# A hybrid block on one core: block inversion two units earlier, ten short-convolution taps inside the delta rule, the long convolution's taps mostly after it, and z in eight buffers

## The chip, the core and the metric

The kernel runs on one core of a Trainium2 chip. The metric is the device time in microseconds (us) from start to end of one execution; lower is better. The five engines are TensorE (PE), VectorE (DVE), ScalarE (ACT), GpSimd (POOL) and SyncE (SP, which only issues the weight loads here).

## The reference, cut to what matters

Two blocks run one after the other on a sequence of 512 tokens of width 1024, all in float32. The first block (feed-forward, sparse and windowed attention, feed-forward) is not touched by the change. The second block has two layers, and each layer computes

```
h    = rms_norm(x)
proj = h @ w_in       # qkv 1536, z_a 512, a 8, b 8, cf_val 512, cf_glu 512, z_b 512, gate 2048
qkv  = silu(conv5(qkv))                       # five taps, depthwise, centred
q, k = l2_normalize(q), l2_normalize(k)
g    = -exp(a_log) * softplus(a + dt_bias);  beta = sigmoid(b)
o    = gated_delta(q, k, v, g, beta) + the same on the reversed sequence
o    = rms(o) * dn_norm_w * silu(z_a);        y_a = o @ w_dn_out
u    = conv31(cf_val * sigmoid(cf_glu)) + cf_conv_b      # 31 taps, depthwise
u    = silu(layer_norm(u)) * silu(z_b);       y_b = u @ w_cf_out
x    = x + (sigmoid(gate_a) * y_a + sigmoid(gate_b) * y_b) @ w_out
```

The gated delta rule needs, for every chunk of 128 tokens and each of four heads and two directions, the inverse of a unit lower-triangular matrix built from the keys, the decays and beta.

## The kernel before, in words

**Units.** All weights are streamed as 300 units of 128x1024 float32 through a ring of four buffers (`raw`). ACT rounds a unit to a high part (`whi`, line 928), POOL makes the low part (`wlo`, line 2027), and PE multiplies with three matmuls for each 128x128 tile (lines 378 to 380): 24 matmuls for a unit of eight tiles. A layer of the second block has 60 units: 8 for the gated linear unit (`glu`) of the long convolution, 12 for qkv, 16 gates, 8 for z, 8 for the two output matrices, 8 for `w_out`.

**Order.** Every engine has its own hand-written program, and engines meet only at semaphores. In a layer, PE does the eight glu units, then the twelve qkv units `j = 0..11` in the order `QKV_ORDER` (keys, queries, values). Each qkv unit lands in one of four PSUM banks; DVE runs its five taps out of that bank into `acc` (lines 1835 and 1838), and ACT applies Silu and, for keys and queries, squares the result; PE adds the squares up over the rows (`sum_rows`, line 405), ACT takes Ln and Exp (`l2_roots`, lines 1186 and 1189), and DVE scales (`unit_length`, line 1768).

**Inversion.** After unit 8 PE forms running sums of the decays and the products of keys by keys (lines 715 to 717 and 689). After unit 10 it spreads the picked decays and beta (`pick`, `pick_b`, lines 727 and 729). DVE then builds 32x32 diagonal blocks (`exponents`, `block_matrices`, from line 1797), and inverts all 32 blocks at once in thirty steps `eliminate(u)` of two small instructions each (lines 1811 and 1813). Between the steps it scales the queries (`u == 8`) and prepares the first decays (`u == 16`, line 1908). `inverse_blocks` (line 1817) and `start_inverse` (line 1932) hand the result to PE, whose first use of it is the transpose of line 835.

**Delta rule.** Meanwhile PE runs six gate units (`LEAD_UNITS`). Then `delta` works through four chunks `i = 0..3`, both directions side by side, and fills PE's waits with tiles of ten more gate units at nine named points of a chunk. DVE has at each of these points a number of taps of the long convolution (`conv(point)`, `POINT_TAPS`). In a chunk with `i > 0`, DVE scales the transposed inverse (line 1956), runs the taps of the point `decay`, and then makes the decayed keys (line 1915), for which PE waits at line 807.

**Long convolution.** 31 taps on four channel groups. The fourth group is ACT's and POOL's (lines 1142 and 2063). The other three, 93 taps, are DVE's (line 1711, each 128x512 out of SBUF): 20 in the glu stage (`GLU_TAPS`), 8 behind the qkv units (`QKV_PHASE_TAPS`), 56 at the points of the four chunks, and 9 behind the last chunk.

**After the delta rule.** PE runs the z units. Behind z unit 0 it sums the convolved rows for the layer norm's mean (line 405, `cu`), behind z unit 1 the squares of `o` and then of the centred `cu`. ACT's Silu of a z unit goes into one of two `prod` buffers, so that ACT waits for `z_used` from the third unit on. z_b comes before z_a, and PE's first output unit in `merge` reads the `cu` half of the rows first.

Of the kernel before, what the change touches and what calls it, by code (L numbers as in the profile page):

```python
# [15 lines left out]
P = 128  # L16
# [42 lines left out]
for _name, _n in (("norm", 8), ("qkv_w", 12 * QKV_TAPS), ("cf_w", 4 * CF_TAPS), ("cf_b", 4), ("ln_w", 4),  # L59
# [95 lines left out]
    "outer": (221824, [P, 256], F32),  # L155
    "fh": (141952, [P, 8, S], F32R),
# [158 lines left out]
POINT_TAPS = {"decay": 2, "level1": 2, "join1": 2, "level2": 1, "join2": 2, "last": 1, "keys": 2, "out": 2}  # L315
LEAD_UNITS = 6
# [48 lines left out]
QKV_PHASE_TAPS = [LATER_TAPS[j:j + 1] if j < 8 else [] for j in range(12)]  # L365
DELTA_TAPS = LATER_TAPS[8:]
# [3 lines left out]
def tensor_engine(pe, m, s):  # L370
# [264 lines left out]
    def merge(g):  # L635
# [4 lines left out]
        for c in range(KD):  # L640
# [4 lines left out]
            for r in (0, 1) if mixer else (1, 0):  # L645
                for k in range(4):
                    if c == 0:
                        pe.wait_ge(s.mix_lo, 8 * g + 4 * (r if mixer else 1 - r) + k + 1)
# [16 lines left out]
    def layer(l):  # L665
# [27 lines left out]
        for j in range(12):  # L693
# [17 lines left out]
            if j == 8:  # L711
# [9 lines left out]
            if j == 10:  # L721
                pe.wait_ge(s.kk_read, 2 * l + 1)
                keys_by_keys(ps[:, 5, :], 3).then_inc(s.d_kk)

                pe.wait_ge(s.picked, l + 1)
                for d in range(2):
                    pe.matmul(ps[:, 6 + d, :], mat(m, "quad"),
                              m.pick[:, 16 * d:16 * d + 16, :].rearrange("p b c -> p (b c)"), start=True, stop=True)
                pe.matmul(ps[:, 4, :], mat(m, "quad"), m.pick_b[:].rearrange("p b c -> p (b c)"), start=True,
                          stop=True).then_inc(s.d_pre)  # L730
        for n in range(LEAD_UNITS):
# [88 lines left out]
    def delta(l):  # L820
# [6 lines left out]
        for i in range(NT):  # L827
# [78 lines left out]
def scalar_engine(act, m, s):  # L906
# [244 lines left out]
    def layer(l):  # L1151
# [23 lines left out]
        def qkv_silu(j):  # L1175
            act.wait_ge(s.qconv, 12 * l + j + 1)
            act.activation(m.qkv[:, QKV_ORDER[j], :], m.acc[:, j % 2, :], ACT.Silu).then_inc(s.qkv)
            if j < 8:
                act.wait_ge(s.qkv, 12 * l + j + 1)
# [17 lines left out]

        for j in range(12):
            weights_upto(u0 + L_QKV + j + AHEAD + 1)
            if j:  # L1200
                qkv_silu(j - 1)
# [15 lines left out]
            if j == 9:  # L1217
                act.wait_ge(s.cum, l + 1)
                cum = m.dsm[:, 0].rearrange("p t (d n) -> p d t n", d=2)
                act.copy(cum, ps[:, 4, 0:32].rearrange("p (d t n) -> p d t n", d=2, t=NT))  # L1220
                act.copy(m.dsm[:, 1], ps[:, 4, 32:64].rearrange("p (t n) -> p t n", t=NT)).then_inc(s.cum_s)
                act.wait_ge(s.d_kk, 8 * l + 2 * l + 1)
                for t in range(3):
                    ins = diagonal_blocks(t, 5 + t)
                ins.then_inc(s.kk_read)
            if j == 11:
                act.wait_ge(s.d_min, 9 * l + 1)
                act.activation(m.blk_l[:], m.blk_l[:], ACT.Exp).then_inc(s.d_dec)
                act.wait_ge(s.d_kk, 8 * l + 2 * l + 2)
                diagonal_blocks(3, 5).then_inc(s.kk_read)  # L1230
        qkv_silu(11)
        for n in range(LEAD_UNITS):
            weights_upto(u0 + L_GATE + n + AHEAD + 1)
            if n == 0:
                l2_roots(4, (0, 1, 2, 3))
# [10 lines left out]
        def z_unit(n):  # L1246
# [3 lines left out]
            if n >= 2:  # L1250
                act.wait_ge(s.z_used, 8 * l + n - 1)
            act.activation(m.prod[:, n % 2, :], ps[:, Z_BANKS[n % 3], :], ACT.Silu).then_inc(s.filled)
# [6 lines left out]
        weights_upto(u0 + L_Z + 1 + AHEAD + 1)  # L1259
        for c in range(4):  # L1260
            act.wait_ge(s.cu_c, 4 * l + c + 1)
            act.activation(m.dl[:, 0, c, :], m.cu[:, c, :], ACT.Square).then_inc(s.cu_sq)
        weights_upto(u0 + L_Z + 2 + AHEAD + 1)
        for c in range(4):
            act.wait_ge(s.o_sums, 4 * l + c + 1)
            act.activation(ps[:, c, :], ps[:, c, :], ACT.Ln, bias=eps, scale=1.0 / P)
        act.wait_ge(s.var, l + 1)
        then(act.activation(ps[:, 5, :], ps[:, 5, :], ACT.Ln, bias=eps, scale=1.0 / (4 * P)))
        for c in range(4):
            act.activation(ps[:, c, :], ps[:, c, :], ACT.Exp, scale=-0.5).then_inc(s.o_root)  # L1270
        act.activation(ps[:, 5, :], ps[:, 5, :], ACT.Exp, scale=-0.5).then_inc(s.root_cu)

        def split_rows(k):
            src = m.o[:, k, :] if k < 4 else m.cu[:, k - 4, :]
            act.wait_ge(s.z_used, 8 * l + (k + 5 if k < 4 else k - 3))
            act.copy(m.fh[:, k, :], src).then_inc(s.mix_hi)

        for n in range(8):
            z_unit(n)
            if n == 1:  # L1280
                for c in range(4):
                    act.wait_ge(s.cu_n, 4 * l + c + 1)
                    act.activation(m.cu[:, c, :], m.cu[:, c, :], ACT.Silu, bias=lcl(m, l, "ln_b", c),
                                   scale=lcl(m, l, "ln_w", c)).then_inc(s.cu_silu)
            if n:
                split_rows(n + 3 if n < 5 else n - 5)
        weights_upto(u0 + L_OUT + AHEAD + 1)
        split_rows(3)
# [13 lines left out]
    def delta(l):  # L1302
# [15 lines left out]
        for i in range(NT):  # L1318
# [4 lines left out]
            for lv in range(1, nl):  # L1323
# [3 lines left out]
                fill(i, f"level{lv}")  # L1327
                fill(i, f"join{lv}")
# [34 lines left out]
def vector_engine(dve, m, s):  # L1363
# [304 lines left out]
    def layer(l):  # L1668
# [153 lines left out]
        for j in range(12):  # L1822
# [459 lines left out]
```

## Time and profile before

| what | value |
|---|---|
| time, median of 3 runs | 2229.32 us (2227.79 to 2230.11) |
| the profiled execution's own time | 2232.36 us |
| its span, first to last instruction | 2231.0 us |
| PE busy | 2091.9 us, 94% of the span |
| DVE busy | 1276.0 us, 57% |
| ACT busy | 873.1 us, 39% |
| POOL busy | 895.9 us, 40% |
| mean granted clock of TensorE | 0.974 of full speed |

The profiled execution is 1.4 us longer than its span and 3.0 us longer than the median of the three runs. Layer 0 of the second block begins near 1240 us of the span and layer 1 near 1740 us; the two look alike instruction by instruction, and times below are of layer 0 unless layer 1 is named. A clock of 1.00 is TensorE's 2.4 GHz, 0.50 is 1.2 GHz.

### The profile page before, as it was taken

Reading aid. Unit: us, or ns where it says so; the run is one execution under the profiler, and the core shown is the slowest. Engines: PE = TensorE matmul, PEld = TensorE weight load, DVE = VectorE, ACT = ScalarE, POOL = GpSimd, SP = SyncE. Lnnn points to the kernel's source line nnn. Section 1 sums busy time; section 2 is a strip of 40 time slices with the busy share of each in tenths; the row PEclk is TensorE's granted clock in tenths of the full one; section 3 lists DMA queues with packets and bytes.
Section 4 is the critical chain, followed back from the end, with each engine's and each line's share of the span. In section 5 each row is a group of like instructions: output and inputs, shape, how many; then the busy total and the mean of one; then the engine's idle time right before and its main releaser. Section 6 shows DMA issues by size and latency. Waiting matters only on the chain.

```text
span 2231.0 us, 26548 instructions
## 1 busy us (share of the span) xinstructions
PE 2091.9 (94%) x10668; PEld 1670.5 (75%) x10668; DVE 1276.0 (57%) x1943; ACT 873.1 (39%) x1404; POOL 895.9 (40%) x431
## 2 busy tenths in 40 slices
PE   7999999989999999999999899889999999799997
PEld 5888787766656788888787677678788777688785
DVE  4422223775677533222225999887543899887543
ACT  4222233313444543222235376344533375343532
POOL 4444443421213344444444454344344454343342
PEclk9999999998999999999999999999999999899999
DMA  4333232320101233333332222100232222010232
GB/s 150 107 132 97 93 95 83 126 66 26 32 22 56 67 98 95 101 95 95 92 96 85 67 76 66 39 25 24 76 95 86 87 83 67 29 30 25 79 96 76
DMA packets 46185, 169.08 MB, mean 76 GB/s; under 512 B 5232, under 2 KB 6000, under 8 KB 45808
## 3 DMA queue, kind: packets, MB, share of 16 engines
q1 hardware_dynamic: 45344, 165.60, 23.9%
q8 instruction: 85, 1.39, 0.3%
q10 hardware_dynamic: 720, 1.79, 0.2%
q14 instruction: 36, 0.29, 0.0%
HBM read 165.27 MB, written 2.10 MB: 75 GB/s over the span
## 4 chain that ended last, share of the span: by engine, by line
PE 71%; DVE 19%; ACT 6%; issue 2%; DMA 1%; POOL 0%; ACTq 0%; DVEq 0%
PE ps L378 20%; PE ps L379 19%; PE ps L380 19%; DVE cu L1711 4%; DVE acc L1838 2%; DVE blk_t L1813 1%; PE ps L405 1%; DVE outer L1811 1%; PE ps L568 1%; PE ps L584 1%; PE ps L553 1%; PE ps L850 1%; PE ps L807 1%; PE ps L497 1%; DVE rt L1694 1%
## 5 line engine op out<-in xcount | busy, mean ns | idle before, releaser
L2027 POOL TENSOR_TENSOR wlo<-raw,whi 128x1024 fp32r<-128x1024 f32 x300 | 739.1, 2470 | 944.6 <-ACT whi L928 943.8
L378 PE MATMUL ps<-xh,whi 128*128 128x512 f32 x1600 | 654.4, 409 | 28.5 <-POOL wlo L2027 17.1
L380 PE MATMUL ps<-xh,wlo 128*128 128x512 f32 x1600 | 628.1, 393 | 0.0
L379 PE MATMUL ps<-xl,whi 128*128 128x512 f32 x1600 | 627.8, 392 | 0.0
L378 PEld LDWEIGHTS ps<-xh,whi 128*128 128x128 f32 x1600 | 303.2, 190 | 116.9 <-issue 28.3
L928 ACT CAST whi<-raw 128x1024 fp32r<-128x1024 f32 x300 | 312.7, 1044 | 190.6 <-DMA raw<-in_stream 190.5
L380 PEld LDWEIGHTS ps<-xh,wlo 128*128 128x128 f32 x1600 | 302.9, 189 | 65.6
L379 PEld LDWEIGHTS ps<-xl,whi 128*128 128x128 f32 x1600 | 303.5, 190 | 64.5 <-issue 7.0
L1711 DVE SCALAR_TENSOR_TENSOR cu<-up,lcols,cu 128x512 f32<-128x512 f32 x180 | 188.4, 1089 | 0.1
L1447 DVE TENSOR_TENSOR ml<-mid,mh 128x512 fp32r<-128x512 f32 x42 | 61.3, 1464 | 164.4 <-ACT mh L984 164.4
L2063 POOL TENSOR_TENSOR cu<-cu,prod 128x512 f32<-128x512 f32 x60 | 87.3, 1455 | 160.5 <-ACT prod L1142 159.3
L378 PE MATMUL ps<-mh,whi 128*128 128x512 f32 x336 | 132.5, 394 | 12.1 <-DVE ml L1447 6.1
L1438 DVE TENSOR_TENSOR ups<-ps,rn 128x512 f32<-128x512 f32 x44 | 30.4, 691 | 194.4 <-PE ps L380 194.4
L974 ACT ACTIVATE sil<-sil 128x512 f32<-128x512 f32 x44 | 27.8, 632 | 285.2 <-DVE sil L1436 285.2
L379 PE MATMUL ps<-ml,whi 128*128 128x512 f32 x336 | 131.9, 393 | 0.0
L380 PE MATMUL ps<-mh,wlo 128*128 128x512 f32 x336 | 131.7, 392 | 0.0
L378 PE MATMUL ps<-fh,whi 128*128 128x512 f32 x256 | 102.3, 400 | 10.7 <-POOL wlo L2027 9.5
L379 PE MATMUL ps<-fl,whi 128*128 128x512 f32 x256 | 100.9, 394 | 0.0
L380 PE MATMUL ps<-fh,wlo 128*128 128x512 f32 x256 | 100.7, 393 | 0.0
L1436 DVE TENSOR_TENSOR sil<-ps,rn 128x512 f32<-128x512 f32 x44 | 30.4, 691 | 117.2 <-PE ps L380 117.1
L378 PEld LDWEIGHTS ps<-mh,whi 128*128 128x128 f32 x336 | 63.8, 190 | 27.0 <-issue 13.7
L378 PE MATMUL ps<-m_y,whi 128*128 128x512 f32 x192 | 74.7, 389 | 0.0
(342 smaller groups left out, 3059.2 us busy)
## 6 DMA issues: line engine op xcount, KB each, us to landing
raw<-in_stream SPq DMA_DIRECT2D x300, 512.0 KB, 3.6
w1k<-in_w SPq DMA_DIRECT2D x1, 2048.0 KB, 8.2
w1v<-in_w SPq DMA_DIRECT2D x1, 2048.0 KB, 10.2
outT<-h SPq DMA_DIRECT2D x4, 512.0 KB, 2.7
h<-in_xT ACTq DMA_DIRECT2D x2, 512.0 KB, 7.7
h<-in_xT SPq DMA_DIRECT2D x2, 512.0 KB, 7.6
mats<-in_mats ACTq DMA_DIRECT2D x1, 448.0 KB, 10.7
msk<-in_masks SPq DMA_DIRECT2D x1, 258.0 KB, 3.9
```

Of the source, the lines that this page charges most:

```text
L378: pe.matmul(out, wh, hi, start=first, stop=False)
L379: pe.matmul(out, wh, lo, start=False, stop=False)
L380: return pe.matmul(out, wl, hi, start=False, stop=last)
L928: act.copy(m.whi[:, slot, :], m.raw[:, slot, :]).then_inc(s.whi)
L974: act.activation(m.sil[:, i % 2, :], m.sil[:, i % 2, :], ACT.Silu).then_inc(s.sil)
L1436: dve.tensor_tensor(m.sil[:, p, :], ps[:, 2 * p, :], m.rn[:], ALU.mult).then_inc(s.g_scaled)
L1438: dve.tensor_tensor(m.ups[:, p, :], ps[:, 2 * p + 1, :], m.rn[:], ALU.mult).then_inc(s.u_scaled)
L1447: dve.tensor_tensor(lo, m.mid[:, i, :], hi.bitcast(F32), ALU.subtract).then_inc(s.ml)
L1711: ins = dve.scalar_tensor_tensor(out=dst, in0=src, scalar=w, in1=dst, op0=ALU.mult, op1=ALU.add)
L1838: ins = dve.scalar_tensor_tensor(out=acc[:, first:last], in0=src[:, first + k - QKV_PAD:last + k - QKV_PAD], scalar=w, in1=acc[:, first:la ...
L2027: pool.tensor_tensor(m.wlo[:, slot, :], m.raw[:, slot, :], m.whi[:, slot, :].bitcast(F32), ALU.subtract).then_inc(s.wlo)
L2063: pool.tensor_tensor(m.cu[:, 3, :], m.cu[:, 3, :], m.prod[:, k % 2, :], ALU.add).then_inc(s.shared)
```

## The change

- Unit 8's PE products move behind unit 7, and those of unit 10 behind unit 8 (the last keys product into bank 3). `pick_rows` moves from behind unit 9's taps to before unit 8's, and `exponents` directly behind unit 8's taps.
- The taps of unit 9 are run inside the elimination at `u == 5`. Units 10 and 11 are copied raw by ACT to their place in `qkv`, and their ten taps run out of SBUF at the points of chunk 0 (`LATE_TAPS`). ACT applies their Silu there.
- Queries are scaled at `u == 12` instead of 8, and the first decays prepared at `u == 20` instead of 16. POOL's identity matrices of chunk 0 move from behind the scaling of the queries to the qkv stage.
- Long-convolution taps: 9 in the glu stage instead of 20, none behind the qkv units instead of 8, 49 at the points of the chunks instead of 56 (chunk 0 gives its first four points to the late taps), and 35 behind the last chunk instead of 9. Together 93 as before.
- In chunks 1 to 3 the decayed keys come before the taps of `decay`.
- z_a comes before z_b, each z unit has its own buffer (`z_o`, `z_cu`), and `merge` reads the `o` half first. The mean of the long convolution is taken behind z unit 3 instead of 0, its variance behind z unit 5 instead of 1.

```diff
@@ constants
+    "z_o": (158336, [P, 4, S], F32),
+    "z_cu": (215680, [P, 4, S], F32),
+LATE_TAPS = {"decay": 2, "level1": 3, "join1": 3, "level2": 2}
+UNIT_Q, DECAY_EXP = 12, 20
@@ tap_plan
-    for c, n in enumerate((1, 2, 10, 7)):
+    for c, n in enumerate((1, 2, 4, 2)):
-QKV_PHASE_TAPS = [LATER_TAPS[j:j + 1] if j < 8 else [] for j in range(12)]
-DELTA_TAPS = LATER_TAPS[8:]
+DELTA_TAPS = LATER_TAPS
@@ PE, layer
-            if j == 8:
+            if j == 7:
                 pe.wait_ge(s.gl, l + 1)
                 pe.wait_ge(s.l2, 8 * l + 4)
...
+            if j == 8:
+                pe.wait_ge(s.qconv, 12 * l + 8)
+                keys_by_keys(ps[:, 3, :], 3).then_inc(s.d_kk)
+                pe.wait_ge(s.picked, l + 1)
+                pe.matmul(ps[:, 4, :], mat(m, "quad"), m.pick_b[:].rearrange("p b c -> p (b c)"), start=True, stop=True)
+                pe.wait_ge(s.kk_read, 2 * l + 1)
+                for d in range(2):
+                    ins = pe.matmul(ps[:, 6 + d, :], mat(m, "quad"),
...
             if j == 10:
-                pe.wait_ge(s.kk_read, 2 * l + 1)
-                keys_by_keys(ps[:, 5, :], 3).then_inc(s.d_kk)
...
+                pe.wait_ge(s.kk_read, 2 * l + 2)
@@ PE, z units
         z_unit(0)
-        pe.wait_ge(s.conv, 3 * l + 3)
-        pe.wait_ge(s.shared, 30 * l + 30)
-        sum_rows(ps[:, 4, :], [m.cu[:, c, :] for c in range(4)]).then_inc(s.mean)
         z_unit(1)
         for c in range(4):
             pe.wait_ge(s.o_sq, 4 * l + c + 1)
             sum_rows(ps[:, c, :], [m.rt[:, c, :]]).then_inc(s.o_sums)
+        z_unit(2)
+        z_unit(3)
+        pe.wait_ge(s.conv, 3 * l + 3)
+        pe.wait_ge(s.shared, 30 * l + 30)
+        sum_rows(ps[:, 5, :], [m.cu[:, c, :] for c in range(4)]).then_inc(s.mean)
+        z_unit(4)
+        z_unit(5)
         pe.wait_ge(s.cu_sq, 4 * l + 4)
...
@@ ACT
+        def raw_values(j):
+            act.wait_ge(s.unit, u0 + L_QKV + j + 1)
+            act.copy(m.qkv[:, QKV_ORDER[j], :], ps[:, j % 4, :]).then_inc(s.qkv)
...
+        qkv_silu(9)
+        raw_values(10)
+        raw_values(11)
@@ DVE, layer
-        for j in range(12):
+        for j in range(9):
             if j == 7:
                 for n in range(4):
                     unit_length(n, (6, 7, 5, 4)[n])
...
+            if j == 8:
+                pick_rows()
+            qkv_taps(j)
...
+        exponents()
         block_matrices()
+        dve.wait_ge(s.cum_s, 3 * l + 2)
+        dve.tensor_scalar(m.dsm[:, 2], m.dsm[:, 2], -1.0, None, ALU.mult).then_inc(s.cum_d)
         for u in range(1, BASE - 1):
             eliminate(u)
-            if u == 6:
...
-            if u == 8:
+            if u == 5:
+                qkv_taps(9)
+            if u == UNIT_Q:
                 for n in range(4):
                     unit_length(4 + n, n)
-            if u == 16:
+            if u == DECAY_EXP:
                 decay_exponents(l, 0)
@@ DVE, delta
+        late = [(j, n) for j in (10, 11) for n in range(QKV_TAPS)]
         def conv(point):
+            if late:
+                for j, n in late[0:LATE_TAPS[point]]:
+                    qkv_tap(j, n)
+                del late[0:LATE_TAPS[point]]
+                return
...
                 if lv == 1:
-                    conv("decay")
                     if i:
                         decayed_keys(l, i)
+                    conv("decay")
```

On DVE, in layer 0, the end of the qkv stage reads before as follows (`pick` and `pick_b` are `pick_rows`, the first group of `acc` is unit 10, the second unit 11, `blk_l` and `blk_t` are the blocks to be inverted):

```order
L1781 TENSOR_TENSOR pick<-dsm,mats 128x512 x2
L1782 TENSOR_TENSOR pick_b<-small,mats 128x512
...
L1835 TENSOR_SCALAR acc<-ps,lcols 128x512
...
L1790 TENSOR_TENSOR blk_l<-dsm,ps 128x512
L1791 TENSOR_TENSOR blk_l<-ps,dsm 128x512
L1792 TENSOR_SCALAR blk_l<-blk_l 128x1024
L1835 TENSOR_SCALAR acc<-ps,lcols 128x512
...
L1797 TENSOR_TENSOR blk_l<-blk_l,small 128x512
L1798 TENSOR_TENSOR blk_l<-blk_l,ps 128x512
L1803 SCALAR_TENSOR_TENSOR blk_l<-kk,blk_l 128x1024
L1804 STREAM_TRANSPOSE blk_t<-blk_l 128x1024
```

In the changed kernel the same place, where the only group of `acc` is unit 8, reads:

```order
L1873 TENSOR_SCALAR acc<-ps,lcols 128x512
...
L1825 TENSOR_TENSOR blk_l<-dsm,ps 128x512
L1826 TENSOR_TENSOR blk_l<-ps,dsm 128x512
L1827 TENSOR_SCALAR blk_l<-blk_l 128x1024
L1832 TENSOR_TENSOR blk_l<-blk_l,small 128x512
L1833 TENSOR_TENSOR blk_l<-blk_l,ps 128x512
L1838 SCALAR_TENSOR_TENSOR blk_l<-kk,blk_l 128x1024
L1839 STREAM_TRANSPOSE blk_t<-blk_l 128x1024
L1905 TENSOR_SCALAR dsm<-dsm 128x32
```

The taps of units 9, 10 and 11 no longer stand ahead of the blocks. On DVE at the end of the last chunk, before (`rt` is the state, `o` the output, `cu` the long convolution), we have:

```order
L1990 TENSOR_TENSOR rt<-rt,ps 128x512
L1711 SCALAR_TENSOR_TENSOR cu<-up,lcols,cu 128x512 x11
L1875 SCALAR_TENSOR_TENSOR cu<-ps,cu 128x512 x4
L1879 SCALAR_TENSOR_TENSOR o<-o,lcols,ps 128x512 x4
L1883 TENSOR_TENSOR cu<-cu,ps 128x512 x4
```

and in the changed kernel:

```order
L2058 TENSOR_TENSOR rt<-rt,ps 128x512
L1746 SCALAR_TENSOR_TENSOR cu<-up,lcols,cu 128x512 x37
L1920 SCALAR_TENSOR_TENSOR o<-o,lcols,ps 128x512 x4
L1942 SCALAR_TENSOR_TENSOR cu<-ps,cu 128x512 x4
L1931 TENSOR_TENSOR o<-o,z_o 128x512 x4
```

There are 37 taps in a row (two of the point `out`, 35 left over) instead of 11, and the centring of `cu`, which needs PE's mean, comes behind the scaling of `o`.

## Rows read from the trace of the kernel before

**Rows 1.** Waits of PE from 1300 us on: total, times, longest.

```profile
PE ps L835 <- DVE dl L1932: 19.6, 2, 10.0
PE ps L807 <- DVE rt L1915: 18.6, 6, 3.1
```

**Rows 2.** PE timeline: start, length, engine, line, operation [idle before, releaser].

```profile
1278.85 0.47 PE L378 MATMUL ps<-xh,whi 128*128 128x512 f32 x1 [1.06 <-POOL wlo L2027]
...
1292.04 1.12 PE L405 MATMUL ps<-rt,mats 128*128 128x512 f32 x2 [2.04 <-ACT rt L1181]
...
1329.59 0.37 PE L715 MATMUL ps<-small,mats 128*128 128x16 f32 x2 [0.22 <-DVE qkv L1768]
...
1344.39 1.16 PE L689 MATMUL ps<-qkv 128*128 128x128 f32 x8 [0.29 <-ACT kk L1195]
...
1371.10 2.07 PE L795 MATMUL ps<-mats,small 128*128 128x128 f32 x8 [2.94 <-DVE qkv L1768]
...
1409.31 1.97 PE L835 MATMUL ps<-mats,dl 128*128 128x128 f32 x8 [9.66 <-DVE dl L1932]
...
1788.73 1.12 PE L405 MATMUL ps<-rt,mats 128*128 128x512 f32 x2
...
1905.77 0.47 PE L835 MATMUL ps<-mats,dl 128*128 128x128 f32 x1 [9.96 <-DVE dl L1932]
```

**Rows 3.** Windows: length, busy PE, PEld, DVE, ACT, POOL, granted clock, DMA.

```profile
1371.00:1377.00 6.00, 5.90 (x27) 5.91 (x28) 5.79 (x8) 0.55 (x1) 3.88 (x2) 0.50 0.04 15
1378.00:1399.00 21.00, 21.00 (x94) 17.37 (x93) 19.93 (x40) 9.57 (x12) 8.01 (x5) 1.00 0.27 75
1451.00:1454.00 3.00, 0.15 (x5) 0.18 (x7) 3.00 (x4) 0.47 (x1) 3.00 (x2) 1.00 0.00 0
...
1532.00:1537.00 5.00, 5.00 (x44) 4.54 (x45) 4.03 (x5) 1.39 (x3) 1.44 (x1) 0.50 0.01 3
```

**Rows 4.** DVE timeline, from the last short-convolution units to the inverse.

```profile
1340.51 3.10 DVE L1838 SCALAR_TENSOR_TENSOR acc<-ps,lcols,acc 128x510 f32<-128x510 f32 x4
...
1357.64 0.68 DVE L1797 TENSOR_TENSOR blk_l<-blk_l,small 128x512 f32<-128x512 f32 x1
...
1372.71 2.40 DVE L1813 TENSOR_TENSOR blk_t<-blk_t,outer 128x198 f32<-128x198 f32 x1
...
1404.35 1.90 DVE L1817 STREAM_TRANSPOSE blk_w<-blk_t 128x1024 f32<-128x1024 f32 x1
```

**Rows 5.** ACT timeline: Silu of unit 5, and Exp of the keys' roots.

```profile
1318.59 0.63 ACT L1177 ACTIVATE qkv<-acc 128x512 f32<-128x512 f32 x1
...
1325.52 2.05 ACT L1189 ACTIVATE ps<-ps 128x512 f32<-128x512 f32 x4
```

**Rows 6.** DVE timeline in chunks 1 (first three) and 3.

```profile
1450.51 2.60 DVE L1711 SCALAR_TENSOR_TENSOR cu<-up,lcols,cu 128x512 f32<-128x512 f32 x2
1453.02 1.28 DVE L1915 SCALAR_TENSOR_TENSOR rt<-ps,dl 128x512 f32<-128x512 f32 x2
...
1459.47 1.35 DVE L1967 COPY_PREDICATED dl<-levels,ps 128x512 f32<-128x512 uint8 x2
...
1538.02 0.69 DVE L1922 TENSOR_TENSOR dl<-ps,dl 128x512 f32<-128x512 f32 x1 [1.46 <-PE ps L850]
```

**Rows 7.** DVE, POOL and PE timelines behind the last chunk.

```profile
1563.63 11.68 DVE L1711 SCALAR_TENSOR_TENSOR cu<-up,lcols,cu 128x512 f32<-128x512 f32 x11
...
1570.38 2.40 POOL L2027 TENSOR_TENSOR wlo<-raw,whi 128x1024 fp32r<-128x1024 f32 x1 [3.08 <-ACT whi L928]
...
1579.36 3.60 PE L405 MATMUL ps<-cu,mats 128*128 128x512 f32 x8
...
1634.67 0.50 PE L378 MATMUL ps<-fh,whi 128*128 128x512 f32 x1 [0.58 <-DVE fl L1895]
```

**Rows 8.** DVE's groups from 1276 to 1361 us: count, busy, mean ns.

```profile
L1711 DVE SCALAR_TENSOR_TENSOR cu<-up,lcols,cu 128x512 f32<-128x512 f32 x15 | 20.2, 1377 | 0.0
```

More of the change, by code:

```diff
@@ L1258, in layer @@
             act.activation(m.rt[:, c, :], m.o[:, c, :], ACT.Square).then_inc(s.o_sq)
-        weights_upto(u0 + L_Z + 1 + AHEAD + 1)
+        z_unit(0)
+        z_unit(1)
+        for c in range(4):
+            act.wait_ge(s.o_sums, 4 * l + c + 1)
+            then(act.activation(ps[:, c, :], ps[:, c, :], ACT.Ln, bias=eps, scale=1.0 / P))
+        for c in range(4):
+            act.activation(ps[:, c, :], ps[:, c, :], ACT.Exp, scale=-0.5).then_inc(s.o_root)
+        z_unit(2)
+        z_unit(3)
@@ L1260, in layer @@
+        weights_upto(u0 + L_Z + 4 + AHEAD + 1)
         for c in range(4):
             act.wait_ge(s.cu_c, 4 * l + c + 1)
[L1262 to L1266, printed above, removed]
+            act.activation(m.rt[:, c, :], m.cu[:, c, :], ACT.Square).then_inc(s.cu_sq)
@@ L1267, in layer @@
+        z_unit(4)
+        z_unit(5)
+        for k in range(4):
+            split_rows(k)
+        weights_upto(u0 + L_Z + 6 + AHEAD + 1)
         act.wait_ge(s.var, l + 1)
         then(act.activation(ps[:, 5, :], ps[:, 5, :], ACT.Ln, bias=eps, scale=1.0 / (4 * P)))
+        act.activation(ps[:, 5, :], ps[:, 5, :], ACT.Exp, scale=-0.5).then_inc(s.root_cu)
+        z_unit(6)
         for c in range(4):
[L1270 removed]
@@ L1271, in layer @@
[L1271 to L1286, printed above, removed]
+            act.wait_ge(s.cu_n, 4 * l + c + 1)
@@ L1287, in layer @@
+            act.activation(m.cu[:, c, :], m.cu[:, c, :], ACT.Silu, bias=lcl(m, l, "ln_b", c),
+                           scale=lcl(m, l, "ln_w", c)).then_inc(s.cu_silu)
+        z_unit(7)
         weights_upto(u0 + L_OUT + AHEAD + 1)
-        split_rows(3)
+        for k in range(4, 8):
+            split_rows(k)
     def decays(l, i):
@@ L1327, in delta @@
                 fill(i, f"level{lv}")
+                if i == 0:
+                    j = 9 + lv
+                    act.wait_ge(s.qconv, 12 * l + j + 1)
+                    act.activation(m.qkv[:, QKV_ORDER[j], :], m.acc[:, j % 2, :], ACT.Silu).then_inc(s.qkv)
                 fill(i, f"join{lv}")
@@ L2063, in shared_tap, with chunk, identities @@
             pool.tensor_tensor(m.cu[:, 3, :], m.cu[:, 3, :], m.prod[:, k % 2, :], ALU.add).then_inc(s.shared)
+    def chunk(l, i):
+        return [(d, 8 * l + 2 * i + d, delta_buffers(m, d), i if d == 0 else NT - 1 - i) for d in range(2)]
+    def identities(l, i):
+        for d, at, b, t in chunk(l, i):
+            if i:
+                pool.wait_ge(s.d_vn, at - 1)
+            else:
+                pool.wait_ge(s.qkv, 14 * l + 1)
+            pool.tensor_copy(b.T, all_heads(mat(m, "ident"))).then_inc(s.d_t0)
     def delta(l):
@@ L2073, in delta @@
         for i in range(NT):
-            both = [(d, 8 * l + 2 * i + d, delta_buffers(m, d), i if d == 0 else NT - 1 - i) for d in range(2)]
-            for d, at, b, t in both:
-                if i:
-                    pool.wait_ge(s.d_vn, at - 1)
-                else:
-                    pool.wait_ge(s.qkv, 12 * l + 12)
-                    pool.wait_ge(s.l2, 8 * l + 8)
-                pool.tensor_copy(b.T, all_heads(mat(m, "ident"))).then_inc(s.d_t0)
+            both = chunk(l, i)
+            if i:
+                identities(l, i)
+            else:
+                pool.wait_ge(s.l2, 8 * l + 8)
             for d, at, b, t in both:
```

183 lines of the change are left out of this document (100 added, 83 removed).

## The prediction

> **What bounds the kernel now.** I read the page for the shares, then PE's waits over the second block, then the timelines of PE and DVE at the places those waits name, then the granted clock around them. PE is busy 94% of the span and the two layers are the only part the change touches, so a gain can only come from PE's idle time there and from the slow clock behind it. The waits show where it sits: 19.6 us in two waits at line 835 for the inverse, and 18.6 us in six waits at line 807 for the decayed keys [rows 1]. The reader is to see that each of the first two is almost 10 us long, one in each layer [rows 2], and that DVE, not PE, ends last there. Smaller ones: 2.94 us at 1371.10 for the scaled queries, 2.04 us at 1292.04 for the first keys' squares, 1.06 us for a weight unit [rows 2]. Idle time costs more than itself: behind the 2.94 us wait the granted clock is 0.50 for at least 6 us, behind a 3.1 us wait of chunk 3 it is 0.50 for at least 5 us, while behind the like wait of chunk 1 it stays 1.00 [rows 3]. A stretch of 5 to 6 us at 0.50 gives away 2.5 to 3 us of PE work.
>
> **Term 1: the inverse is ready earlier.** In full stretches PE runs 94 recorded matmuls in 21 us [rows 3]; a few records are missing, so I take 5.45 us for a unit of 24. A row sum adds 0.9 us (8 records in 3.6 us [rows 7]), so a unit with one takes 6.35.
> Eleven long-convolution taps leave the glu stage and eight the qkv stage. DVE is then free when unit 0 ends and follows PE instead of trailing it, so the waits of 2.04 and 1.06 us go, and unit 2 ends at 1292.04 - 2.04 - 1.06 = 1288.9. Units 3 to 5 with their sums end at 1308.0; the fourth sum and unit 6 make 1314.3, unit 7 1319.8.
> The keys must now be scaled behind unit 7, one unit sooner. A unit's five taps take 3.10 us for four [rows 4] and about 0.75 for the first: 3.85. Unit 5's taps end at 1311.9. From its Silu to the end of the roots' Exp ACT takes 1327.57 - 1318.59 = 9.0 us [rows 5], so the roots are there at 1320.9. DVE's four scalings then end between 1321.5 and 1323; I take 1322.4. PE waits 2.6 us where it waited 0.22 [rows 2]. Behind it stand units 8 to 11 and everything else.
> Then, on PE: from 1329.59 to 1344.39 stand the products and two units less 0.29 us of wait [rows 2], so the products take 3.6 us: 1326.0. Unit 8: 1331.5. The last keys product (1.16 us [rows 2]) and three 128x512 products of two passes at 0.9 each: 1335.4. On DVE three instructions of about 0.65 each make the exponents: 1337.4. ACT's table load and Exp, which I estimate from the four-instruction Exp of 2.05 us [rows 5] at 2.4 together, end at 1339.8. So `block_matrices` starts at 1339.8 where it started at 1357.64 [rows 4].
> From there to the transposes of line 1817 DVE took 1404.35 - 1357.64 = 46.7 us [rows 4]. The change adds unit 9's taps, 3.85. It also adds a wait: at u = 12 the queries need roots whose sums stand behind gate unit 0. PE reaches those at 1335.4 + 4 x 5.45 = 1357.2, sums 3.1 us, ACT about 4 us for Ln and Exp, so the roots come near 1363, and I take 2 us of wait, less about 1 us of an old wait for small exponentials. The transposes start at 1339.8 + 46.7 + 3.85 + 1 = 1391.4, and line 835 runs 4.96 us after them as before [rows 2, 4]: 1396.3 instead of 1409.31. **Gain in layer 0: 13.0 us.** PE itself, with gate units 1 to 5 and the first products, arrives near 1391 to 1393, so the wait shrinks to some 3 to 5 us and DVE remains the bound.
> Layer 1: unit 2 ends at 1788.73 with no wait behind DVE [rows 2]. The same 107.4 us lead to 1896.1 instead of 1905.77: **9.7 us.** Together 22.7. The new 2.6 us wait at unit 7 lies between the 2.04 us behind which no slow stretch followed and the 2.94 us that had one; at even odds of losing 2.5 us it costs 1.2 a layer. **Term 1: -20.** Bounds: -28 with no wait at u = 12 and no slow clock, -12 when every GpSimd instruction meets an elimination step. Such a step takes 2.40 us instead of 0.4 [rows 4], and with PE running on there are two or three more weight units inside the elimination than before, 2 us each.
>
> **Term 2: the chunks.** Putting the decayed keys first brings PE's line 807 forward by the two taps, 2.60 us [rows 6], out of 3.1 [rows 1]. I do not book 6 x 2.5 us. In chunk 1 DVE runs from 1450.51 to the copy at 1459.47 without idle [rows 6]; the same instructions stand in that stretch after the swap, so PE waits for that copy (at line 842) instead. Only in chunks 2 and 3 has DVE something to win: there PE came back at 0.50 and DVE in turn waited, 1.46 us at 1538.02 [rows 6] and smaller pieces. That is 2 to 3 us a chunk if the moved wait, now about 2.3 us, leaves the clock alone, and nothing if it doesn't. In chunk 0 DVE has ten short taps where it had seven long ones at the first four points; three more at 0.75 us are 2.3 us, but there too it waited for a slow PE. The V transposes' new wait is for a Silu beside the copy of the inverse and costs under 0.5. I take -2.5 a layer: **Term 2: -5**, bounds -12 and +4.
> Here the Trainium skill, page "SBUF — State Buffer", section "Who interferes with whom", speaks against the change: a VectorE instruction with two SBUF inputs and a GpSimd instruction that reads SBUF exclude each other for the whole instruction, while one with a single SBUF input is not held up. The trace agrees: a POOL instruction of 2.40 us stands beside an elimination step of 2.40 instead of 0.4, and four taps out of PSUM take 3.10 everywhere. The ten late taps of a layer have left PSUM for SBUF. If three of them met a weight unit, at 2.0 us each, term 2 would be +7 for both layers instead of -5.
>
> **Term 3: behind the last chunk.** 37 taps instead of 11. Eleven took 11.68 us from 1563.63, 1.06 each, with two POOL instructions of 2.40 among them [rows 7]. POOL has one weight unit for each PE unit here, so I keep 1.06: 39.3 us, to 1603.0. PE has 18 gate tiles and z unit 0, which end at 1579.36 [rows 7], then z1 (5.45), the sums of `o` (3.2), z2 and z3 (10.9): 1599. It waits about 4 us for the convolution, long enough, by the 2.94 us case, for a slow stretch: 2.5. Then mean 3.1, z4 and z5 10.9, variance 3.2, z6 and z7 10.9: 1603.0 + 28.1 + 2.5 = 1633.6. The first output unit takes 5.45, and waits for the `cu` half: ACT has to finish z7 and a weight cast before it splits, which I put at 1.5 us. It ends at 1640.5. Before, its last tile of 0.68 us began at 1634.67 after 0.58 us of wait [rows 7]: 1635.4. Loss 5.1 us a layer, and half a us for the likelier DVE hold-ups. **Term 3: +11**, bounds +4 (POOL spares the taps, no slow clock) and +18. The eight z buffers are worth the two waits of about 1 and 0.58 us that z units and `merge` had, already inside this sum. Moving POOL's identity copies and reordering z_a and z_b cost nothing: their cover is PE's own units, and without it they would cost the 1.2 us of the copy.
>
> **Sum.** -20 - 5 + 11 = -14. The profiled execution took 2232.36, so 2218 for its like. It lies 3.0 us above the median of the runs shown, so the median should be about **2215 us**.
>
> **The rivals.**
> - *More of it arrives.* The moved waits of about 2.3 us leave the clock at 1.00, as the 3 us of chunk 1 did [rows 3], and the roots don't hold DVE: term 1 -25, term 2 -9, term 3 +9, so 2204. The long slow stretches behind chunk 2 and 3 speak against it.
> - *The start is not gained.* PE's products behind unit 7 wait for ACT's chain, and extra weight units hold the elimination, so that line 835 comes only 7 us sooner in each layer: -14, -2, +12, so 2225. For it: the 2.40 us step [rows 4]. Against: 17.8 us of head start at `block_matrices` stand against 3.85 us of added work.
> - *Slower: the tail becomes the bound.* Everything behind the last chunk waits on the 37 taps. In the qkv stage a tap of the same shape took 1377 ns on average [rows 8], because POOL does its long-convolution adds besides the weights. At that rate 37 taps take 51 us, 11.6 more a layer: 2215 + 23 = 2238. Each 0.1 us a tap is 3.7 us a layer; the change turns to a loss above 1.06 + 14/74 = 1.25 us a tap. Against: POOL's adds for the long convolution are over by then, and the eleven taps behind the last chunk measured 1.06.
> - *It does nothing*, because both gains were cover for DVE work that must be done anyway: DVE does the same work in all, but 57% of the span leaves it idle time, above all behind the chunks, where it waited in the z units. This shares the 2225 to 2234 region with the second rival.
>
> **How the numbers follow.** Near 2215 (2209 to 2221): 0.42. More (2198 to 2209): 0.27. Little at the start (2221 to 2234): 0.22, of which somewhat less than half lies within 0.2% of 2229.3, that is above 2224.9; 0.2% is about what a measurement of this kernel can tell from no change. Slower: 0.09, 0.02 of it from stacked waits short of the tail rival. So faster 0.81, same 0.10, slower 0.09. The range leaves out most of the slow rival and the far end of the fast one: 2202 to 2226.
>
> **What would show it.** Right: PE's wait at the inverse's transposes falls from 9.7 us to 3 to 5 and starts some 13 us (layer 0) and 10 us (layer 1) sooner; a wait of 2 to 3 us behind unit 7; waits near 2.3 us at the second-level transposes instead of 3.1 at the first products in chunks 1 to 3; a PE wait near 4 us before the sum of `cu`. Wrong: an elimination that takes over 52 us, a tail whose taps take other than about 1.06 us, or slow stretches inside the chunks where there was none.

## The result, and the profile after

The changed kernel takes 2237.54 us (median of 18 runs, 2230.25 to 2240.13) and the kernel before, on the same chips, 2229.72 us (18 runs, 2222.76 to 2234.12). The ratio is 1.0031, interval 1.0023 to 1.0040: **slower by 0.3%**, where 2215 us and faster was forecast. The median lies outside the range of 2202 to 2226.

The profiled execution of after took 2233.95 us, 3.6 below its own median, and that of before was 2.6 above its. The two traces differ by only 1.7 us of span, so I read from them where time moves, and take how much from the ratios. PE's waits from 1240 us on: total, times, longest. ([rows 1] counts from 1300 us; its two figures are the same from 1240.)

```profile
PE ps L859 <- DVE dl L2035: 25.3, 7, 4.1
...
PE ps L384 <- ACT sg L1168: 6.0, 2, 3.0
PE ps L852 <- DVE dl L1992: 5.9, 4, 2.1
PE ps L721 <- DVE qkv L1803: 4.7, 2, 2.4
PE ps L384 <- DVE fl L1937: 4.3, 4, 1.9
PE ps L824 <- DVE rt L1975: 3.5, 6, 0.6
```

Line numbers have moved: 835 is now 852, 842 is 859, 807 is 824, and the tap's line 1711 is 1746. The two waits at the inverse fell from 19.6 to 5.9 us and the six at the decayed keys from 18.6 to 3.5. A wait that hardly existed has taken their place: 25.3 us at line 859, the second-level transposes, for DVE's copy at line 2035 (line 1967 before). The 6.0 us at line 384 behind ACT are new too: only 0.5 us stood there before.

PE's timeline at the places that the prediction named, to be held against [rows 2] and [rows 7]:

```profile
1286.86 1.02 PE L411 MATMUL ps<-rt,mats 128*128 128x512 f32 x2
...
1320.17 0.37 PE L721 MATMUL ps<-small,mats 128*128 128x16 f32 x2 [2.36 <-DVE qkv L1803]
...
1384.39 0.47 PE L384 MATMUL ps<-xh,whi 128*128 128x512 f32 x1 [2.98 <-ACT sg L1168]
...
1397.53 0.66 PE L852 MATMUL ps<-mats,dl 128*128 128x128 f32 x4 [2.01 <-DVE dl L1992]
1400.29 1.11 PE L852 MATMUL ps<-mats,dl 128*128 128x128 f32 x4 [2.10 <-DVE dl L1992]
...
1452.90 1.94 PE L859 MATMUL ps<-mats,dl 128*128 128x128 f32 x8 [4.08 <-DVE dl L2035]
...
1598.25 2.31 PE L411 MATMUL ps<-cu,mats 128*128 128x512 f32 x5
...
1631.76 0.75 PE L384 MATMUL ps<-fh,whi 128*128 128x512 f32 x1 [1.90 <-DVE fl L1937]
```

PE's transposes of the inverse (line 852) start at 1397.53 instead of 1409.31. At 1598.25 PE reaches the sum of `cu` without waiting. What happens between is in the windows of chunks 1, 2 and 3, first the kernel before, then after. Columns: length, then busy time and count of PE, PEld, DVE, ACT, POOL, then granted clock, DMA.

```profile
1444.08:1482.39 38.31, 34.85 (x313) 30.65 (x312) 32.74 (x55) 17.49 (x31) 17.15 (x11) 1.00 0.08 28
1482.39:1522.21 39.82, 36.35 (x313) 32.04 (x312) 32.59 (x55) 17.48 (x31) 16.96 (x11) 0.96 0.09 28
1522.21:1561.18 38.97, 35.52 (x303) 31.41 (x302) 31.45 (x53) 16.86 (x30) 14.68 (x8) 0.91 0.09 28
```

```profile
1434.73:1477.57 42.84, 37.15 (x314) 32.42 (x312) 35.42 (x55) 17.48 (x31) 16.50 (x11) 0.92 0.08 25
1477.57:1518.91 41.34, 36.32 (x313) 31.72 (x312) 34.63 (x55) 17.48 (x31) 16.79 (x11) 0.96 0.09 27
1518.91:1560.30 41.39, 35.70 (x304) 30.98 (x303) 34.15 (x53) 16.88 (x30) 14.13 (x8) 0.92 0.09 26
```

DVE runs the same 55, 55 and 53 instructions and is busy 7.4 us longer with them. In chunk 1 the clock falls from 1.00 to 0.92 besides; in chunks 2 and 3 it is as before. The DVE timeline of chunk 1 shows which instructions grew; [rows 6] has the same place before.

```profile
1439.96 1.28 DVE L2024 TENSOR_TENSOR dl<-ps,small 128x512 f32<-128x512 f32 x2
1441.16 1.28 DVE L1975 SCALAR_TENSOR_TENSOR rt<-ps,dl 128x512 f32<-128x512 f32 x2
1442.35 7.11 DVE L1746 SCALAR_TENSOR_TENSOR cu<-up,lcols,cu 128x512 f32<-128x512 f32 x4
...
1452.04 1.33 DVE L2035 COPY_PREDICATED dl<-levels,ps 128x512 f32<-128x512 uint8 x2
```

And POOL's timeline of after, beside it:

```profile
1440.24 2.53 POOL L2161 TENSOR_TENSOR dl<-dl,qkv 128x512 f32<-128x512 f32 x2 [9.80 <-ACT dl L1326]
1442.72 2.81 POOL L2095 TENSOR_TENSOR wlo<-raw,whi 128x1024 fp32r<-128x1024 f32 x1
1445.70 3.22 POOL L2131 TENSOR_TENSOR cu<-cu,prod 128x512 f32<-128x512 f32 x2 [0.17 <-ACT prod L1161]
```

Four taps take 7.11 us in one run. POOL works from 1440.24 to 1448.92 with 0.17 us of pause, first the scaled queries, then a weight's low part, then two of its own long-convolution adds. Before, the like adds stood elsewhere, behind the taps, beside DVE's scores:

```profile
1449.59 2.96 POOL L2084 TENSOR_TENSOR dl<-dl,qkv 128x512 f32<-128x512 f32 x2 [9.79 <-ACT dl L1296]
1452.52 2.80 POOL L2027 TENSOR_TENSOR wlo<-raw,whi 128x1024 fp32r<-128x1024 f32 x1
1457.56 3.13 POOL L2063 TENSOR_TENSOR cu<-cu,prod 128x512 f32<-128x512 f32 x2 [2.25 <-ACT prod L1142]
```

From the scaled queries to the adds are 7.97 us before and 5.46 after: with the keys first PE's products are ready sooner, ACT's behind them, and POOL's adds wait only for ACT.

By stages the traces say, after minus before, both layers: to the inverse -17.0 (10.5 and 6.5, counted from the start of the layer's own work, since the two executions were 1.3 us apart there already), chunk 0 +4.4, chunks 1 to 3 +12.7, tail +2.8.

### The profile page after: what moved, and what is told of

It is laid out like the page before. It is cut to its first block, busy times and chain, and to the rows that moved or that the text cites. A ratio compares the mean times of both kernels' runs of the same rounds, so it can differ in the third digit from the quotient of the medians.

```text
span 2232.7 us, 26560 instructions
## 1 busy us (share of the span) xinstructions
PE 2091.1 (94%) x10668; PEld 1668.5 (75%) x10668; DVE 1285.8 (58%) x1943; ACT 896.8 (40%) x1424; POOL 894.5 (40%) x431
## 4 chain that ended last, share of the span: by engine, by line
PE 74%; DVE 16%; ACT 7%; issue 1%; DMA 1%; POOL 0%; ACTq 0%; DVEq 0%
PE ps L384 21%; PE ps L386 20%; PE ps L385 20%; DVE cu L1746 2%; PE ps L411 1%; PE ps L574 1%; PE ps L590 1%; PE ps L559 1%; DVE blk_t L1848 1%; DVE outer L1846 1%; DVE acc L1876 1%; PE ps L503 1%; ACT whi L947 1%; DVE rn L1434 1%; ACT dl L1368 1%
## 5 line engine op out<-in xcount | busy, mean ns | idle before, releaser
L1746 DVE SCALAR_TENSOR_TENSOR cu<-up,lcols,cu 128x512 f32<-128x512 f32 x180 | 193.0, 1126 | 0.1
## 6 DMA issues: line engine op xcount, KB each, us to landing
mats<-in_mats ACTq DMA_DIRECT2D x1, 448.0 KB, 10.5
```

Source lines behind the costliest of these rows:

```text
L1746: ins = dve.scalar_tensor_tensor(out=dst, in0=src, scalar=w, in1=dst, op0=ALU.mult, op1=ALU.add)
```

## The experiments

Theory A: the taps collide with POOL's instructions because the swap leaves four of them in one run. Theory B changes with the experiment: in x1 and x2 the order of the two calls costs nothing, and the late taps or the moved inversion cost the time; in x3 and x9 four taps in one run hold PE up whatever POOL does. Against both stands the forecast's slower rival, the tail. Each kernel's ratio is to the kernel before on the same chip.

**x1: after, the two calls swapped back.**

```
                 if lv == 1:
-                    if i:
-                        decayed_keys(l, i)
                     conv("decay")
+                    if i:
+                        decayed_keys(l, i)
```

> The changed kernel with one part undone: in chunks 1 to 3 the taps of point decay stand ahead of the decayed keys again. Theory A (collision): in the changed kernel the four taps of decay and level1 run together and take 7.11 us where they took 2.60 and 2.30 apart, because the instruction that reads PSUM no longer stands beside POOL's work; undoing it gives about 2 us back in each of six chunks, so about 12 us less than the changed kernel: near 2225 us, or 0.998 of before, with PE's wait back at the first products (3.1 us) and gone from the second-level transposes. Theory B (the late taps or the moved inversion cost it): the order of these two is neutral, the time stays within 2 us of the changed kernel (2235 to 2239, 1.003) and only the place of the wait moves.

2220.95 us, ratio 0.9969 (0.9956 to 0.9982). DVE's timeline of the chunk and PE's wait at the decayed keys are those of before again:

```profile
1438.68 2.59 DVE L1746 SCALAR_TENSOR_TENSOR cu<-up,lcols,cu 128x512 f32<-128x512 f32 x2
1441.19 1.27 DVE L1975 SCALAR_TENSOR_TENSOR rt<-ps,dl 128x512 f32<-128x512 f32 x2
1442.39 2.30 DVE L1746 SCALAR_TENSOR_TENSOR cu<-up,lcols,cu 128x512 f32<-128x512 f32 x2
...
PE ps L824 <- DVE rt L1975: 18.6, 6, 3.1
```

Four taps in 4.89 us instead of 7.11. Without the swap the change is faster by 0.3%.

**x2: before, with the swap alone** (the same edit the other way).

> The kernel before with that one part alone: decayed keys ahead of the taps of decay in chunks 1 to 3. Theory A: the four taps take about 7.1 us instead of 4.9, PE waits about 4 us at the second-level transposes, and the kernel becomes about 8 to 13 us slower than before (1.004 to 1.006). Theory B: no change (0.999 to 1.001). My prediction's own step would have it 5 us faster (0.998).

2247.26 us, ratio 1.0088 (1.0072 to 1.0105): the swap costs 19.6 us in the old kernel, more than the 8 to 13 that theory A expected. Line 807 loses 15.1 us of wait, line 842 gains 24.5, and line 879 goes from 2.1 to 7.2.

```profile
1452.14 7.11 DVE L1711 SCALAR_TENSOR_TENSOR cu<-up,lcols,cu 128x512 f32<-128x512 f32 x4
...
PE ps L842 <- DVE dl L1967: 24.5, 6, 4.1
...
PE ps L807 <- DVE rt L1915: 3.5, 6, 0.6
```

**x3: after, POOL's adds at later points** of each chunk.

```
-SHARED_POINTS = ("level1", "join1", "level2", "join2", "values")
+SHARED_POINTS = ("join2", "last", "keys", "values", "out")
```

> The changed kernel with ACT's and POOL's adds of the fourth channel group moved from the points level1, join1, level2, join2, values to join2, last, keys, values, out. Theory A: with POOL's adds away from it the run of four taps falls from 7.11 to about 5.5 us (POOL's product with the queries and its weight unit remain), PE's wait at the second-level transposes from 4.1 to about 2.5, and the kernel gains 6 to 10 us on the changed one (about 2229, 1.000), unless the adds collide as badly at their new places. Theory B: the run of four taps is long for another reason, and stays at 7 us; no gain.

2225.38 us, ratio 0.9987 (0.9975 to 0.9998). With only the end of the scaled queries and the weight beside them, the four taps take 5.02 us, and the wait at line 859 is halved:

```profile
1443.99 5.02 DVE L1746 SCALAR_TENSOR_TENSOR cu<-up,lcols,cu 128x512 f32<-128x512 f32 x4
...
PE ps L852 <- DVE dl L1992: 15.8, 10, 2.1
PE ps L859 <- DVE dl L2035: 12.0, 6, 2.0
...
PE ps L824 <- DVE rt L1975: 6.8, 6, 1.1
```

But the waits at lines 852 and 824 grew, and over the whole trace these three lines add up to 34.6 us, against 34.7 in after. In chunks 1 to 3 of both layers PE's waits sum to 28.1 us, 3.9 less than in after, while the chunks are 8.4 us shorter. The rest goes with the clock: no single wait there is above 2.0 us instead of 4.1, and the granted clock of the three chunks of layer 0 is 1.00, 1.00 and 0.96 where after has 0.92, 0.96 and 0.92.

**x9: x3 with the calls swapped back,** the fourth corner of the square.

> x3 (POOL's long-convolution adds at later points) with the two instructions swapped back: taps ahead of the decayed keys. It is the fourth corner of a square: swapped or not, POOL's adds early or late. With the adds early the swap cost 16.6 us in the changed kernel (x1 against after). If that cost is the four taps meeting POOL's adds (theory A), the swap is worth little or something with the adds late: PE's waits of 2.0 us at the second-level transposes turn into 3.1 us at the half-level products, chunks become about 1 us longer than x3's 40.4, and the kernel is 0 to 7 us slower than x3: 2225 to 2232. If the swap costs by itself, whatever POOL does (theory B: four taps in one run hold up PE), x9 is some 10 us or more faster than x3: 2215 or below.

2233.73 us, ratio 1.0021 (1.0010 to 1.0033). PE waits 21.8 us at line 824, 3.7 at most, and 11.1 at line 852. At 2229.7 us for before, the square reads: adds early, taps first 2222.8; adds early, keys first 2236.6; adds late, taps first 2234.4; adds late, keys first 2226.8. The swap costs 13.8 us with the adds early and gains 7.6 with them late. Theory B falls. The traces agree: chunks 1 to 3 of both layers together take 238.3, 253.1, 257.0 and 244.7 us, in the same order. Here too the clock carries most of it: x9's chunks are 12.4 us longer than x3's and hold only 2.8 us more of wait, but in layer 0 they run at 0.92, 0.96 and 0.92.

Late adds are not free themselves, and with the taps first they cost 11.6 us. In x3 and x9 POOL's last add of a chunk stands ahead of its identity copies for the next one, and DVE waits 1.71 us for them at 1437.92 (x3) and 1434.92 (x9). In chunks 1 to 3 of x9 PE then waits 7.5 us at line 852, where x1 has no such wait, and 3.2 us more than x1 at line 824, with the lower clock besides. That these waits make up the whole cost is not shown.

**x4: after, with no tap at the two early points** and six at `keys`, behind the last level.

```
-POINT_TAPS = {"decay": 2, "level1": 2, ..., "keys": 2, "out": 2}
+POINT_TAPS = {"decay": 0, "level1": 0, ..., "keys": 6, "out": 2}
```

> The changed kernel with the four taps of decay and level1 moved to the point keys in chunks 1 to 3 (in chunk 0 only the taps behind the late ones change), where DVE waits 4 us for PE. The number of taps is the same. Both theories agree that these taps are on the path ahead of the second-level transposes: the copy there comes 4 to 7 us sooner, the waits of 4.1 us go, and with them the slow clock behind them. Six times 3 to 4.5 us: 2210 to 2219 us, 0.992 to 0.995 of before, unless six taps at keys outlast DVE's 4 us of idle time, which would give back about 1 us a chunk.

2196.43 us, ratio 0.9855 (0.9836 to 0.9874), the fastest of all: 32 us under before, and below the 2210 to 2219 that was expected. Its chunks:

```profile
1435.06:1470.82 35.76, 34.81 (x313) 30.66 (x312) 31.41 (x55) 17.50 (x31) 17.68 (x11) 1.00 0.10 30
1470.82:1506.57 35.75, 34.81 (x313) 30.66 (x312) 31.40 (x55) 17.50 (x31) 17.67 (x11) 1.00 0.10 31
1506.57:1540.50 33.93, 32.99 (x304) 29.09 (x303) 30.23 (x53) 16.88 (x30) 13.72 (x8) 1.00 0.10 32
```

PE is busy 34.8 of 35.8 us, and the clock is 1.00 throughout. In chunk 1 the same 55 instructions keep DVE busy for 31.4 us, 4.0 less than in after. Six taps at `keys` run unhindered:

```profile
1461.31 4.05 DVE L1746 SCALAR_TENSOR_TENSOR cu<-up,lcols,cu 128x512 f32<-128x512 f32 x6
```

That is 0.68 us a tap, so the four of after lost 7.11 - 2.70 = 4.4 us to POOL and the four of before 4.90 - 2.70 = 2.2.

**x5: before, with the same table of taps.**

> The kernel before, with the same table of tap places as x4: no tap at decay and level1, six at keys. Before, chunks 1 to 3 took 38.3, 39.8 and 38.8 us in layer 0, and x4's took 35.8, 35.8 and 33.9. If the four early taps are what holds a chunk in the kernel before as well (theory T), its chunks become as short as x4's: about 4 us each, 24 us in both layers, so near 2205, and x4 stays 7 to 10 us below it, which is what the change's start and tail are worth without the swap. If x4's gain is only the collision taken away, which the kernel before does not have (theory S), this table moves it by less than 5 us: 2223 to 2230.

2206.93 us, ratio 0.9891 (0.9876 to 0.9906), with chunks of 35.8, 35.8 and 33.9 us. 24 us lay open in the old kernel without any of this change. x4 is 0.0036, or 8 us, below it: what the start and the tail of the change are worth when nothing collides. The forecast's first and third terms had -20 + 11 = -9.

**x6: x4 with the old places of the early taps.**

```
-    for c, n in enumerate((1, 2, 4, 2)):
+    for c, n in enumerate((1, 2, 10, 7)):
...
+            if j < 8:
+                cf_tap(*LATER_TAPS[j])
```

> x4 with the old places of the early long-convolution taps: ten and seven in the last two glu units instead of four and two, and one behind each of the first eight qkv units. The tail falls from 33 taps to 14. The taps that leave the tail ended there 5 us before PE came to the sum of cu, so they give nothing back. At the start the waits behind DVE in units 0 to 2 return, about 3 us in layer 0, and DVE reaches the keys' scaling later. Theory of the trace (tail is covered): 3 to 9 us slower than x4, 2199 to 2205. Theory of the prediction (tail costs 5.5 us a layer): the trade is about even or x4 loses up to 6 us: 2190 to 2198.

2212.72 us, ratio 0.9918 (0.9903 to 0.9933), 14 us slower than x4 and so beyond both ranges. The tail went from 33 taps to 14, and in layer 0 the time from the last output product to the first result of `merge` stayed at 75.75 us. The start paid for all of it: PE waits 10.9 us in two waits for the keys' scaling, where x4 has 4.7, and 4.0 in three waits for the keys' squares, where x4 shows none.

```profile
PE ps L721 <- DVE qkv L1803: 10.9, 2, 5.8
```

**x8: x4 with a longer tail,** `keys` 2 instead of 6.

> x4 with two taps at keys instead of six and none added elsewhere: four taps fewer in every chunk, 16 more behind the last chunk (49 instead of 33 in each layer). In x4 33 taps took 30.55 us, 0.93 each, and ended at 1573.5; PE came to the sum of cu at 1578.5. By that rate 16 taps are 14.8 us, less 5.0 us of room: PE waits 9.8 us in each layer, 20 us in both, and 0 to 5 us of slow clock: 2216 to 2221. By the prediction's 1.06 us a tap the 49 take 52 us: 13 to 14 us of wait a layer and 5 of slow clock: 2227 to 2230. If the chunks also gain from having fewer taps, up to 5 us less in each case.

2213.07 us, ratio 0.9920 (0.9905 to 0.9934). DVE's tail, and PE's sum of `cu`:

```profile
1545.88 41.15 DVE L1746 SCALAR_TENSOR_TENSOR cu<-up,lcols,cu 128x512 f32<-128x512 f32 x49
...
1587.08 3.77 PE L411 MATMUL ps<-cu,mats 128*128 128x512 f32 x4 [5.51 <-DVE cu L1746]
```

49 taps are 0.84 us each, less than either rate that I had expected with. PE could have begun at 1581.57, which is 35.7 us behind the first tap: some 42 taps fit. The four matmuls behind the wait take 3.77 us at a mean granted clock of 0.52, where five took 2.31 in after: the wait costs clock too. A tail that is too long does set the end, but the change's 37 taps are not too many.

**x7 and x10: x4 with chunk 0's exponents at step 16 and at step 24** of the elimination instead of 20.

```
-UNIT_Q, DECAY_EXP = 12, 20
+UNIT_Q, DECAY_EXP = 12, 16
```

> x4 with chunk 0's decay exponents at step 16 of the elimination instead of 20. In x4 and in after a gate unit waits 3.0 us behind ACT because the exponents come late. If the inverse alone sets the end of that stretch, this wait is only moved to the inverse's transposes: within 1.5 us of x4's 2196. If the wait also costs clock or delays something behind it, 2 to 6 us faster.

> x4 with chunk 0's decay exponents at step 24 of the elimination instead of 20 (x7 had 16, and its inverse came 4 us later though the same instructions ran: seven of the elimination's instructions took 2.3 to 2.5 us instead of 0.2 to 0.4, beside POOL's weights, where x4 had five). If where the steps fall against POOL's instructions is what decides (theory L), the place of the exponents moves the inverse by 2 us steps in no set direction: 2190 to 2204. If earlier exponents are better for the gate unit that waits for them and later ones worse (theory G), it is 2 to 5 us slower than x4: 2198 to 2201, with a gate unit's wait behind ACT longer than 3.0 us.

x7: 2203.47 us, 0.9874 (0.9857 to 0.9890). x10: 2205.56 us, 0.9893 (0.9874 to 0.9911). x10 loses 8 us to x4. x7's 4 us are no more than the two intervals leave open, but in its trace the transposes of the inverse come 3.9 us later after the keys' scaling than in x4 (2.6 in layer 1), though DVE runs the same instructions. It had been expected level with x4 or faster. DVE's and POOL's timelines of x7 say why:

```profile
1383.76 2.42 DVE L1846 TENSOR_TENSOR outer<-blk_t 128x168 f32<-128x168 f32 x1
1386.21 2.41 DVE L1848 TENSOR_TENSOR blk_t<-blk_t,outer 128x168 f32<-128x168 f32 x1
...
1390.33 2.45 DVE L1848 TENSOR_TENSOR blk_t<-blk_t,outer 128x108 f32<-128x108 f32 x1
...
1395.80 2.29 DVE L1846 TENSOR_TENSOR outer<-blk_t 128x30 f32<-128x30 f32 x1
...
1383.46 4.97 POOL L2095 TENSOR_TENSOR wlo<-raw,whi 128x1024 fp32r<-128x1024 f32 x2 [8.38 <-ACT whi L947]
1390.25 2.40 POOL L2095 TENSOR_TENSOR wlo<-raw,whi 128x1024 fp32r<-128x1024 f32 x1 [1.82 <-ACT whi L947]
...
1395.69 2.34 POOL L2095 TENSOR_TENSOR wlo<-raw,whi 128x1024 fp32r<-128x1024 f32 x1 [0.53 <-ACT whi L947]
```

One of DVE's instructions stretches over each of POOL's four. In x10 the elimination has little of this (its 60 instructions are busy 27.1 us, 31.5 in x4 and 37.5 in x7), and a gate unit waits 6.1 us for the late exponents instead. So both theories of x10 were half right, and its time lies above the range of either. The collisions set when the inverse is ready. But PE's two waits behind ACT grow from 6.0 to 12.2 us and those at line 859 in chunk 0 from 0.8 to 5.3, and only the 5.9 us at line 852 are gone.

## Why the prediction was wrong

**Term 1, the inverse: right.** -20 forecast, -17.0 in the traces. `block_matrices` starts at 1339.56 (forecast 1339.8), DVE's transposes of the inverse at 1390.62 (1391.4), in a trace whose layer 0 began 1.3 us earlier, and PE waits 2.36 us at unit 7 (2.6). One wait was in no term: 2.98 us at 1384.39, and 3.00 in layer 1, where a gate unit waits for ACT, which works behind chunk 0's exponents. It is gone in x7, with the exponents at step 16, and doubled in x10. The wait at the inverse is the shorter for it: 2.01 us where 3 to 5 was forecast. Line 852 follows 6.9 us behind instead of 4.96 in layer 0, because `start_inverse` itself, 1.3 us elsewhere, takes 4.43 beside POOL's scaled queries (from 1394.19 to 1396.88) and its weight at 1397.25. The second direction then waits another 2.10 us at 1400.29, and 1.03 in layer 1, which is most of the 4.4 us that chunk 0 lost and which no term had. x6 shows that the taps gone from the start are worth 14 us.

**Term 2, the chunks: the step that failed.** -5 forecast with bounds of -12 and +4; the chunks cost 17.1 us in the traces, 12.7 of them in chunks 1 to 3. The mechanism of the moved wait was right, and x3 against x9 shows its worth with the adds out of the way: a wait of 2.0 us (forecast 2.3), a clock of 1.00 in four of the six chunks, and a gain of 7.6 us. What failed is the sentence that "the same instructions stand in that stretch after the swap". The same instructions did, but I kept their durations, 2.60 and 2.30 us for the pairs of taps, and those were no property of a tap. They were what two taps take beside POOL's scaled queries, and two beside the end of a weight, with the keys (out of PSUM) standing beside the rest of it. The swap moves the keys away from the weight and puts taps there, and by hurrying PE and ACT it pulls POOL's adds forward into the same run. The wait became 4.1 us instead of 2.3. One of the seven waits at line 859, of 0.8 us, lies in chunk 0 of layer 1. So in chunks 1 to 3 the waits at lines 859 and 824 grew by 24.5 + 3.5 - 18.6 = 9.4 us, and the slower clock and the rest are 3.3. x1, x2 and the square show this step alone: in the new kernel it turns the sign of the whole change, and in the old one it costs 19.6 us.

The Trainium skill, page "SBUF — State Buffer", section "Who interferes with whom", states that a VectorE instruction with two SBUF inputs and a GpSimd instruction that reads SBUF exclude each other. The trace agrees, with 7.11 us for four taps that take 2.70 undisturbed. I had weighed the rule for the ten late taps, and those were mostly spared: a late unit's four taps at 1403.03 took 3.11 us. One thing was wrong in that weighing: the first tap of a unit has a single SBUF input and was taken as safe, yet at 1411.05 it took 1.06 us beside one of POOL's adds, and 0.47 at 1402.52 with none beside it. Where the hold-up struck was the long-convolution taps, which had always had two SBUF inputs.

**Term 3, the tail: right in sign, mis-sized.** +11 forecast with bounds of +4 and +18, +2.8 measured. The 37 taps took 33.18 us, 0.90 each and not 1.06, and ended at 1595.93, before PE came at 1598.25. So no wait and no slow clock stood there; `merge` waits 1.90 us (1.5 forecast). The 1.06 came from eleven taps with two POOL instructions among them; the 37 had five, and none from 1582.79 to 1593.12. The slower rival, this tail as the bound, is not what happened: x8 puts its edge at some 42 taps, and x6 gains nothing by a shorter one. The kernel is slower by another mechanism.

**Sum.** -17.0 + 17.1 + 2.8 = +2.9 in the layers, less the 1.3 us of their start: 1.6, and the spans differ by 1.7. The medians differ by 7.8; the other 6 us are how these two executions lie to their medians (3.6 and 2.6). With the swap left out the forecast would have read -20 + 11 = -9, and x1 measures 0.0031, -7 us.

## What to carry to other kernels

A duration read from a trace holds only beside what ran beside it: before two instructions change places, write down what POOL does beside both places, and which of its work the swap itself will bring forward. Work that can run at any time belongs where nobody waits for its engine: moving four such taps a chunk out of the path to the copy was worth 24 us in the old kernel, more than the whole change had aimed at. How long the single waits are counts beside their sum: in chunks 1 to 3 x3 waits 3.9 us less than after and takes 8.4 us less. An experiment on one swapped line in both kernels settles such a cost at once, and a square of two edits shows whether it is theirs or between them.

## What the runs showed of the hardware

- A vector instruction with two SBUF inputs that meets a POOL instruction lasts about as long as what is left of it, however small it is: 128x30 elements took 2.29 us beside a POOL instruction of 2.34, and 0.21 elsewhere (x4's elimination has such steps at 0.21).
- The hold-up also reached instructions that I had counted as safe: two predicated copies took 4.43 us beside POOL's scaled queries and a weight of 2.40, and 1.34 in chunk 1.
- A wait of 4.08 us had a mean granted clock of 0.57 behind it, over 5.6 us; where the longest waits were 2.0 us (x3) chunks 1 to 3 of layer 0 ran at 1.00, 1.00 and 0.96, and where they were 3.1 us (x1) at 0.96, 0.96 and 1.00. Where all were under 1 us (x4) they ran at 1.00. The wait's row of after:

```profile
1452.90:1458.50 5.60, 5.60 (x36) 4.40 (x38) 3.62 (x6) 2.46 (x4) 0.00 (x0) 0.57 0.00 0
```
